# A two-block transformer kernel in split single precision: output projections begun inside the mixers' last steps, small input blocks multiplied in the split format

## The reference

```python
# block 1, layer 0 (even): gated linear attention on 4 heads + softmax attention on 8 query heads
gq, gk, gv, gog, gz, aq, ak, av = _split(h @ w_in, (256, 256, 512, 512, 32, 512, 128, 128))
o = concat([gated readout of the 4 linear heads, attention output of the 8 heads])   # 512 tokens x 1024
x = x + m[2] * _rms(o @ even_w_out)
# block 1, layer 1 (odd): 8 recurrent heads of width 128, latent tokens only
o = _gated_readout(...)                                                             # 256 tokens x 1024
x = x + m[2] * _rms(o @ odd_w_out)
# block 2, layer 0: latent attention (8 heads) + retention (8 heads)
z = h @ w_in_2            # 416 columns (256 query, 128 key-value, 32 rotary), then 4 x 512 for retention
x = x + m[2] * (concat([attention, retention]) @ w_out_2)
```

## Time and profile before

| | us |
|---|---|
| median of 3 runs (lowest, highest) | 2678.09 (2676.75, 2680.05) |
| the profiled execution: its own time | 2671.8 |
| its span, first to last instruction | 2670.0 |
| busy PE / DVE / ACT / POOL in the span | 2380.8 / 1469.1 / 1029.8 / 208.2 |
| mean granted clock of PE (1 is 2.4 GHz) | 0.953 |

### The profile page before, as it was taken

The page is one execution under the profiler, slowest core; times in us unless marked ns, Lnnn a source line. Parts: engine busy times, 40 slices in busy tenths (PEclk is TensorE's granted clock), DMA queues, the critical chain, the costliest instruction groups (busy, mean ns, idle before and its releaser), DMA issues.

```text
span 2670.0 us, 35094 instructions
## 1 busy us (share of the span) xinstructions
PE 2380.8 (89%) x14650; PEld 1856.3 (70%) x14650; DVE 1469.1 (55%) x2319; ACT 1029.8 (39%) x1736; POOL 208.2 (8%) x294
## 2 busy tenths in 40 slices
PE   5987788999997988868997988979999998979899
PEld 3834455888884766658996843347787787758899
DVE  5416745555555387775455315545565554871454
ACT  3233434222234355544444325644322224321543
POOL 0001200000000033330000002200201100000110
PEclk8988989999998999988998999989999999989899
DMA  7235641534421554324542224432443333252443
GB/s 267 76 132 199 251 159 50 167 140 142 156 87 64 149 167 158 127 105 152 186 170 102 93 79 136 164 111 90 141 154 139 139 126 135 108 202 95 157 168 134
DMA packets 172478, 372.25 MB, mean 139 GB/s; under 512 B 7040, under 2 KB 99456, under 8 KB 158112
## 3 DMA queue, kind: packets, MB, share of 16 engines
q1 hardware_dynamic: 172320, 370.01, 39.4%
HBM read 339.55 MB, written 30.44 MB: 139 GB/s over the span
## 4 chain that ended last, share of the span: by engine, by line
PE 73%; DVE 13%; ACT 7%; issue 3%; DMA 2%; POOL 1%; SPq 0%; DVEq 0%; ACTq 0%; POOLq 0%
PE ps L169 72%; DVE sb_R L200 5%; ACT sb_R L248 2%; DVE sb_WP L200 1%; DVE sb_H L200 1%; DMA sb_R<-mod_w 1%; DVE sb_R L232 1%; DMA sb_slot<-mod_w 1%; DVE sb_X L217 1%; PE ps L179 1%; DVE sb_cst L214 1%; DVE sb_cst L200 1%; ACT sb_R L254 1%; ACT L244 1%; DVE sb_R L229 1%
## 5 line engine op out<-in xcount | busy, mean ns | idle before, releaser
L169 PE MATMUL ps<-sb_HP,sb_WP 128*128 128x512 f32 (+1 forms) x5568 | 1049.7, 350 | 68.8 <-DVE sb_WP L200 39.7
L169 PEld LDWEIGHTS ps<-sb_HP,sb_WP 128*128 128x128 f32 x5568 | 898.3, 194 | 208.6 <-issue 46.6
L200 DVE TENSOR_TENSOR sb_WP<-sb_slot,sb_WP 128x1024 fp32r<-128x1024 f32 x356 | 438.3, 1237 | 633.4 <-ACT sb_WP L254 633.3
L254 ACT ACTIVATE sb_WP<-sb_slot 128x1024 fp32r<-128x1024 f32 x356 | 374.1, 1057 | 788.0 <-PE ps L169 777.4
L169 PE MATMUL ps<-sb_XP,sb_WP 128*128 128x512 f32 (+1 forms) x2592 | 452.5, 337 | 10.2 <-DVE sb_XP L200 10.2
L169 PEld LDWEIGHTS ps<-sb_XP,sb_WP 128*128 128x128 f32 x2592 | 399.7, 190 | 62.9 <-DVE sb_XP L200 12.2
L200 POOL TENSOR_TENSOR sb_R<-sb_R 128x128 f32<-128x128 f32 (+2 forms) x194 | 153.7, 815 | 1829.3 <-ACT sb_R L248 1401.8
L169 PE MATMUL ps<-sb_R 128*32 128x64 f32 (+8 forms) x2088 | 172.7, 288 | 64.9 <-DVE sb_R L200 29.9
L200 DVE TENSOR_TENSOR sb_R<-sb_R 128x256 f32<-128x256 f32 (+3 forms) x398 | 201.7, 541 | 30.4 <-ACT sb_R L248 27.3
L169 PEld LDWEIGHTS ps<-sb_R 128*32 128x32 f32 (+5 forms) x2088 | 123.5, 152 | 122.6 <-issue 66.1
L248 ACT ACTIVATE sb_R<-ps 128x512 f32<-128x512 f32 (+1 forms) x208 | 99.4, 514 | 128.4 <-PE ps L169 124.9
(11 more groups left out here) (137 smaller groups left out, 1952.8 us busy)
## 6 DMA issues: line engine op xcount, KB each, us to landing
sb_slot<-mlp_w SPq DMA_DIRECT2D x32, 2048.0 KB, 9.1
sb_slot<-mod_w SPq DMA_DIRECT2D x22, 2048.0 KB, 8.1
sb_R<-ada_w SPq DMA_DIRECT2D x12, 2048.0 KB, 7.5
sb_slot<-ada_w SPq DMA_DIRECT2D x24, 1024.0 KB, 4.8
sb_slot<-ffn_w_gate SPq DMA_DIRECT2D x22, 1024.0 KB, 5.3
sb_slot<-ffn_w_up SPq DMA_DIRECT2D x22, 1024.0 KB, 7.8
sb_slot<-ffn_w_down SPq DMA_DIRECT2D x10, 2048.0 KB, 7.7
sb_slot<-odd_w_in SPq DMA_DIRECT2D x32, 512.0 KB, 7.1
```

The lines of the kernel that those rows point to most:

```text
L169: return self.e.matmul(out, w, x, start=start, stop=stop, skip_group_check=True)
L200: return BLANK if self.e is None else self.e.tensor_tensor(out, a, b, op)
L254: return self.e.activation(out, a, ACT.Copy) if scale is None else self.e.activation(out, a, ACT.Copy, scale=scale)
```

## The change

- `Projections`: the rest is gone. Its columns form a narrow block (`narrow_pe`) that is loaded, split and multiplied as the others are, so there are five loads and 20 pieces. In Even it stands third, in Mla second; the load of Even's writes the key columns twice into the slot, so that each key group is one block of 128 output rows. In Mla the last 32 columns come out of a block of 96. The order of Even's other blocks changes.
- `four_pe` and `tokens4_pe` take each bank right before its first matmul instead of all four at once.
- `OutProj` has no fence. A row waits for its own weight piece, its own split activation tile (`ready`) and, as each tile's turn comes, its bank. Rows go in an `order` in which their inputs are done. In Even and Mla, ACT and DVE split the first three weight pieces and five or six of the activation tiles at the ends of the last three steps (`EARLY`), each behind the waits of `place_free`; PE's rows stand behind its last instruction of the mixer.
- In Odd, rows 0 to 6 run beside the mixing of head 7, one in each of its first seven steps and ahead of that step's mixing products; pieces 0 to 2 are split at the end of head 6. The eight output tiles share four banks (0, 5, 1, 2) in pairs; row 0 opens each bank with matmuls over all 512 columns, whose second half is zeros. The sum of squares goes to bank 4 and the next norm's to bank 3.
- The output matrices' loads are four DMAs of 512 KB instead of one of 2 MB.

```diff
-        self.x, self.bank = x, 6 if x is None else 0
+        self.x, self.bank = x, 6 if x is None else 0 if x[0] != "odd.res" else 3
...
+        self.bank = 0 if down.banks is None else 4
+        self.copied = 0 if down.banks is None and not down.add else None
...
 def four_pe(p, pe, pieces, x, n, u, cols):
-    bs = [pe.take() for _ in range(4)]
+    bs = []
...
-        for a, (b, ps) in enumerate(bs):
+        for a in range(4):
+            if k == 0:
+                bs.append(pe.take())
+            b, ps = bs[a]
...
+def narrow_pe(p, pe, pieces, u, blocks):
+    bs = []
+    for k in range(KT):
+        if k % 2 == 0:
+            y = next(pieces)
+            pe.wait_ge("w", y)
+            w = p.wp(y % 4)
+        pe.wait_ge("hp", k)
+        for a, (kind, c0, m, at, _) in enumerate(blocks):
+            if k == 0:
+                bs.append(pe.take())
+            b, ps = bs[a]
+            cut = [z[:, 512 * (k % 2) + c0:512 * (k % 2) + c0 + m] for z in w]
+            if kind == "tokens":
+                i = pe.mm3(ps[:, 0:m], [p.HP[:, z, k, 128 * at:128 * at + 128] for z in range(2)], cut, k == 0, k == KT - 1)
+            else:
+                i = pe.mm3(ps[0:m, :], cut, p.hp(k, T), k == 0, k == KT - 1)
+            if k == KT - 1:
+                i.then_inc(*pe.sig("out", u, a, bank=b))
+                pe.until(b, "taken", u, a)
...
+    def at(self, t):
+        if self.banks is None:
+            return self.p.ps[t][:, 0:self.n]
+        return self.p.ps[self.banks[t // 2]][:, 256 * (t % 2):256 * (t % 2) + self.n]
+    def row_pe(self, pe, k, y, ts=tuple(range(KT))):
+        p, c, last = self.p, self.c, k == self.kt - 1
+        pe.wait_ge("w", y)
+        pe.wait_ge("xp", c, k)
+        w = p.wp(y % 4)
+        for t in ts:
+            at, x, first = self.at(t), self.bufs[k % len(self.bufs)], k == 0
+            if first and self.banks is None:
+                pe.vacant(t)
+            elif first and t % 2 == 0:
+                pe.vacant(self.banks[t // 2])
+                at, x = p.ps[self.banks[t // 2]], p.hp(k, T)
+            i = pe.mm3(at, [z[:, 128 * t:128 * t + 128] for z in w], x, first and (self.banks is None or t % 2 == 0), last)
...
 class OutProj:
...
+        self.pieces = Pieces(p, self.name, out_loads(W, order))
+        self.pieces.prior, self.pieces.free = prior, free
+        self.down = Down(p, 0, KT, nt, lambda k: MIX[:, order[k], :], [p.hp(k, nt) for k in range(KT)], p.room2(0, KT, nt),
+                         last=norm, resid=None if norm else (n0, 1, mods), banks=banks)
...
+    def some_act(self, act, pieces, blocks):
+        act = act.on(self.name)
+        for x in pieces:
+            self.pieces.act_part(act, x)
+        for k in blocks:
+            self.down.act_part(act, k, self.ready)
+    def some_dve(self, dve, pieces, blocks):
+        dve = dve.on(self.name)
+        for x in pieces:
+            self.pieces.dve_part(dve, x)
+        for k in blocks:
+            self.down.dve_part(dve, k)
+    def row_pe(self, pe, k):
+        ts = tuple(range(KT)) if k or self.down.banks else (3, 4, 5, 7, 0, 1, 2, 6)
+        self.down.row_pe(pe.on(self.name), k, k, ts)
...
-        e.fence(*self.before)
-        self.down.act(e, self.pieces.act_ahead(e), lambda *_: None)
+    def act(self, act, x0, k0):
+        for k in range(KT):
+            self.some_act(act, [k] if k >= x0 else [], [k] if k >= k0 else [])
+        self.down.end_act(act.on(self.name))
...
-        rest_load = [(lambda s: view(s)[:, :, 0:32], W[:, 1536:1568].rearrange(rows, p=128)),
-                     (lambda s: view(s)[:, :, 32:288], W[:, 2080:2336].rearrange(rows, p=128))]
+        cut = lambda c, n: lambda s: view(s)[:, :, c:c + n]
+        narrow = [(cut(0, 32), W[:, 1536:1568].rearrange(rows, p=128)), (cut(32, 64), W[:, 2080:2144].rearrange(rows, p=128)),
+                  (cut(96, 128), W[:, 2080:2208].rearrange(rows, p=128)), (cut(224, 192), W[:, 2144:2336].rearrange(rows, p=128))]
         self.proj = Projections(
-            p, "even.in", W, (0, 512, 1568, 1024), mods,
-            [("features", [(q[:, 0, :], ACT.Copy, 0.125), (q[:, 1, :], ACT.Copy, 0.125), (k[:, 0, :], ACT.Copy, 1.0), (k[:, 1, :], ACT.Copy, 1.0)]),
+            p, "even.in", [block_load(W, 1568), block_load(W, 0), (4096, narrow)] + [block_load(W, c0) for c0 in (512, 1024)], mods,
+            [("features", [(self.aq[:, m, :], ACT.Copy, 1.0) for m in range(4)]),
+             ("features", [(q[:, 0, :], ACT.Copy, 0.125), (q[:, 1, :], ACT.Copy, 0.125), (k[:, 0, :], ACT.Copy, 1.0), (k[:, 1, :], ACT.Copy, 1.0)]),
+             ("narrow", [("features", 0, 32, 0, self.z[0:32, :])] + [("features", 32 + 128 * g, 128, 0, kk[:, g, :]) for g in range(2)]
+              + [("tokens", 288, 128, j, va[:, j, :]) for j in range(4)]),
              ("tokens", [(self.vg[:, j, :], ACT.Copy, 1.0) for j in range(4)]),
-             ("features", [(self.aq[:, m, :], ACT.Copy, 1.0) for m in range(4)]),
-             ("features", [(self.og[:, m, :], ACT.Silu, 1.0) for m in range(4)])],
-            rest_load,
-            [("features", 0, 32, 0, self.z[0:32, :])]
-            + [("features", 32 + 64 * g, 64, 64 * half, kk[64 * half:64 * half + 64, g, :]) for g in range(2) for half in range(2)]
-            + [("tokens", 160, 128, j, va[:, j, :]) for j in range(4)], view)
+             ("features", [(self.og[:, m, :], ACT.Silu, 1.0) for m in range(4)])])
...
+        done = [("even.gla", ("o", (h // 2, h % 2))) for h in range(4)] + [("even.att", ("att", 0, m)) for m in range(4)]
+        order = (0, 1, 4, 5, 6, 2, 3, 7)
+        self.out = OutProj(p, "even", io["even_w_out"][0], p.H, 0, True, mods, order,
+                           lambda e, k: e.wait_ge(*done[order[k]][1], of=done[order[k]][0]), free=self.place_free)
...
+    def place_free(self, e, x):
+        for h in range(2):
+            e.wait_ge(*("o", (1, h)) if x == 3 else ("values", 1, h), of="even.gla")
...
+    EARLY = ((0, 1), (0, 1)), ((2,), (2, 3)), ((), (4,))
...
+            if s >= self.steps - 3:
+                self.out.some_act(act, *self.EARLY[s - self.steps + 3])
+        self.out.act(act, 3, 5)
...
+        self.out = OutProj(p, "odd", p.io["odd_w_out"][0], MIX, TC, True, mods, tuple(range(8)),
+                           lambda e, k: e.wait_ge("o", k, of="odd.mix"), self.pieces, banks=(0, 5, 1, 2))
...
+    def out_pe(self, pe):
+        for k in range(7):
+            self.out.row_pe(pe, k)
+            yield
+    def out_first(self, some, e):
+        for _ in range(8):
+            yield
+        for x in range(3):
+            some(e, (x,), ())
+            yield
+    def out_act(self, act):
+        self.out.some_act(act, (), (0,))
+        for k in range(7):
+            self.out.some_act(act, (k + 3,), (k + 1,) if k < 6 else ())
+            yield
+    def out_dve(self, dve):
+        e = dve.on("odd.out")
+        e.wait_ge("made", 7, 3, of="odd.in")
+        e.fill(self.p.HP[:, :, 0, TC:T].bitcast(F32)).then_inc(*e.sig("zeros"))
+        self.out.some_dve(dve, (), (0,))
+        for k in range(7):
+            self.out.some_dve(dve, (k + 3,), (k + 1,) if k < 6 else ())
...
+            if h == 7:
+                pe.on("odd.out").wait_ge("zeros")
+            together(self.project_pe(pe, h + 1) if h < 7 else self.out_pe(pe), self.mix_pe(pe, h), self.read_pe(pe, h - 1), steps(more, 11))
         together(self.read_pe(pe, 7), more)
-        self.out.pe(pe)
+        self.out.pe(pe, 7)
...
+            together(self.pieces_act(ahead) if h < 7 else self.out_act(act), *([self.out_first(self.out.some_act, act)] if h == 6 else []),
+                     self.mix_act(act, h), self.cross_act(act, h), self.read_act(act, h - 1),
                      *([self.project_act(act, h + 1)] if h < 7 else []), steps(more, 11))
         together(self.read_act(act, 7), more)
-        self.out.pieces.act_first(act)
-        self.out.act(act)
+        self.out.act(act, 10, 7)
...
+            p, "mla.in", [block_load(W, 416), (4096, narrow)] + [block_load(W, c0) for c0 in (928, 1440, 1952)], mods,
+            [("features", cp(self.rq)),
+             ("narrow", [("features", 128 * m, 128, 0, self.cq[:, m, :]) for m in range(2)]
+              + [("features", 256, 128, 0, self.ckv), ("features", 320, 96, 64, self.kr[64:96, :])]),
+             ("features", cp(self.rk, 0.125)), ("tokens", cp(self.rv)),
+             ("features", [(self.rg[:, m, :], ACT.Silu, 1.0) for m in range(4)])], ("ffn1.res", "x"))
...
+        order = (0, 4, 1, 5, 2, 6, 3, 7)
+        self.out = OutProj(p, "mla", io["w_out_2"][0], p.H, 0, False, mods, order,
+                           lambda e, k: e.wait_ge(*done[order[k]][1], of=done[order[k]][0]), free=self.place_free)
+    EARLY = ((0,), (0, 1)), ((1,), (2, 3)), ((2,), (4, 5))
+    def place_free(self, e, x):
+        last = len(self.attend.units) - 1
+        e.wait_ge(*(("s", 0, last), ("s", 0, last), ("pv", 0, last - 1), ("pv", 0, last))[x], of="mla.lat")
```

(36 more changed lines are left out.)

190 lines of the change are left out of this document (79 added, 111 removed).

## The result

The changed kernel takes 2655.63 us (median of 4 runs, 2653.83 to 2659.77) against 2677.42 for the kernel before: ratio 0.9921, 95% interval 0.9904 to 0.9939, so 16 to 26 us off. Forecast were 2629, at most 2650. The sign was right; 26.6 of the forecast 48 us are missing.

A forecast was written before the change was run, and what follows sets the result against it. PE was taken as the bound (73% of the last-ending chain), through costly matmuls and late inputs. Terms 8.7 + 5.3 + 2.3 + 9.2 + 9.4 + 14.3 = 49.2 us off the profiled 2671.8 gave 2622.6, as median 2629 us; range 2616 to 2650.

The forecast's parts named there:

- The narrow blocks: Even's and Mla's remaining projection columns as fp32r matmuls from split weights: 8.7 us off in Even, 5.3 in Mla.
- dear tokens: Rival, chance 0.30: in Even's narrow block a 128-column fp32r matmul costs as much as the float32 one; 2640 us.
- Banks one by one: After the first half of Squared 0, PE starts the next product once one bank is free, not four: 2.3 us off.
- Mla's output: Output rows start right after Mla's last mixing matmul, ending at 1819.3 against 1828.8: 9.4 us off, bounds 3 and 10.
- Even's output: Output rows follow Even's mixer without the gap, at a full clock: 9.2 us off, bounds 3 and 9.9.
- Now row 0 follows that last matmul: Step for Even: its first output row starts at the mixer's last PE matmul, where it started at 387.0 after 379.3.
- Odd's output: Rows beside head 7 shorten the end by 23.8 us and lengthen the head by 9.5: 14.3 us off, bounds 1 and 16.
- only row 7 remains behind o(7): Step for Odd's end: one output row is left after head 7's output, ending 5.9 us behind it; 23.8 us off.
- issue ahead of their use; zero: The output matrices' smaller DMAs move the same bytes early enough to cost nothing, else a few tenths.
- S: Growth of Odd's head 7 from the output rows beside it: 9.5 us, between 7.9 and 23.
- The prediction's own sign: Check in Odd: head 7's level products end near 1198 on the old time scale, PE above 90% busy there.
- head 7 pays: Rival, chance 0.15: PE and DVE wait for each other each step, head 7 grows nearly 20 us, Odd gives 4; 2639.

The follow-up runs named there:

- e8: The kernel of e1 with none of Mla's output splits early, all behind the mixer: 2649.31 us, 8.3 us over e1.
- e6: The kernel of e1 with the tile of bank 7 last in row 0 of Even's and Mla's output: 2634.09 us, 7.0 us under e1.
- e1: The changed kernel with the next stage's first two weight loads put on SP's queue ahead of the fence on odd.mix: 2641.05 us.
- e5: The kernel of e1 with Odd's output weight pieces beside head 7 split a step later and each step's tile ahead of its piece: 2635.12 us.
- e11: The kernel of e9 with PE's rows beside head 7 one step later and the wait for the zeros right ahead of row 0: 2627.13 us.
- e3: The changed kernel with Odd's output back behind its mixer, eight rows into eight banks, still without the fence: 2644.81 us.
- e4: The kernel before with only the narrow blocks of Even and Mla from the change: 2660.51 us against 2677.57.
- e9: The changed kernel with the edits of e1, e5 and e6 together: 2631.07 us.

## Why the prediction was wrong, step by step

**The narrow blocks** (8.7 + 5.3): right, 17 us with an interval of 13 to 20. The choice between 0.116 and 0.23 us for a 128-wide fp32r matmul was the largest doubt in the sum, and the rival "dear tokens" (0.30) is out: 0.121. Even's narrow block took 8 x 3.38 = 27.0 us, where 27.4 was written.

**Banks one by one** (2.3): the wait is 0.33, so 2.35 off. Right in the trace, not run alone.

**Mla's output** (9.4): 9.2 in the trace behind the last product, 1.0 given back in the mixer; e8 shows that the early splits carry it.

**Even's output** (9.2): 3.5 (5.4 less 1.9). The step that failed is "Now row 0 follows that last matmul", which priced when row 0 starts, and not its eight banks. DVE's queue had been looked at for its readouts ("DVE's last readout falls some 5 us later"), and not for its fold of bank 7, which stands in the same queue. e6 shows it: 4.3 us in the trace. Of the 5.7 us missing here some 1.1 are the mixer, which grew by 1.9 where 0.8 was taken.

**Odd's output** (14.3): it cost 11. Two steps failed.

First, "After: only row 7 remains behind o(7) ... end at o(7) + 5.9; 23.8 us off". The rows did end there, 6.5 us behind o(7), and in e1 the stretch from o(7) on falls from 45.4 to 20.7 us, the 23.8 and a little more. What comes after them was taken to move with them, and it did not: the next stage's weights stand on SP's queue behind a fence on o(7), and the rows had been their cover (13.4 us from issue to the end of the wait, once under 29.8 us of rows, now under 6). e1 shows it: 14.6 us. The prediction said of the output loads that they "issue ahead of their use; zero", and asked nothing of the loads behind them. No rival had this mechanism, and it alone puts the time past the range.

Second, S = 9.5, measured 20.2. The sum was made per engine ("so its sum asks for 6.4 + 1.5 more: less than PE's", of DVE). It left out that the engines wait for each other. Of PE's 37.6 us from row 0 to the last level product, forecast 28: 6.9 more for rows (28.4 against 21.5, three of them at a mean granted clock of 0.63), 4.6 of waits between steps, 1.9 less for the head's own products; and row 0 started 2.9 us later than worked out, of which 1.5 had been set apart for the pieces in head 6. The prediction's own sign, level products that end near 1198 on the old scale with PE above 90% busy, reads 1209 and 88%. e5 takes 4.5 us of head 7, 3.0 of them by the clock of two rows, and e11 2.9 more by freeing the diagonal product from row 0 and the zeros. The rival "head 7 pays", with S near 20, had named it with 0.15, and gave Odd 4 us: with e1's queue Odd gives 3.8, if loosely. A forecast of head 7 alone should have had this as the likeliest. About 12 us of growth are left in e11 (50.9 against 38.4 in e3), near the 9.5; that these are PE's own work was not tried by an experiment.

**What adds up.** 14.6 (e1) + 5.6 (e5) + 5.4 (e6) = 25.6 of the missing 26.6. Each size is loose by 2 to 4 us, since the intervals are that wide, and e4's 3 us over its forecast hides a like amount elsewhere; that the three together bring the time to 2631 is measured (e9). That this lies 2 us from the forecast is in part luck: head 7 is still 15.4 us longer in e9 than in e3, where S was 9.5, and the 3 us by which the narrow blocks gave more than forecast stand against it.

## What to carry to other kernels

Work that is moved ahead leaves bare what it covered: for every microsecond taken off a stretch, list the loads that were landing under it, and where their issue stands in its queue. A fence in a DMA queue holds back everything behind it, wanted or not. When rows of one matrix are threaded through a chain on another engine, price the loop (row end, place free, copy, subtract, next row), not only each engine's sum; and check each resource of the first row, every bank and who reads it last, not only its first input.
